# Sample attention's value products moved from ahead of the prompt's attention into two of its steps

## What is computed

```python
logits = jnp.einsum('btngd,btknd->btngk', qg, k_sel) * (HEAD_DIM ** -0.5)
bias = rel_bias[t5_bucket(qpos[None, :, None] - idx)]
logits = jnp.where(valid, logits + bias, -jnp.inf)
p = jax.nn.softmax(logits, axis=-1)
o = jnp.einsum('btngk,btknd->btngd', p, v_sel)
# samples: v_all = concatenate([cache_v[page_table], v]) of 512 + 1 rows, 8 heads, 2 key heads
xs = xs + merge(cy, gc, o, ga, w_out)
```

## Time and profile before

| | us |
|---|---|
| median of 3 runs | 1704.01 |
| lowest, highest | 1702.09, 1707.3 |
| the profiled execution, its own time | 1701.9 |
| span of the profiled execution | 1700.2 |
| PE busy | 1513.3 (89%) |
| DVE, ACT, POOL busy | 1003.3, 697.9, 415.0 |

### The profile page before, as it was taken

One profiled execution on the slowest core, in us unless ns is written; L12 is line 12 of the kernel. 1 busy time (PEld: TensorE's weight loads), 2 busy tenths in 40 slices (PEclk: granted clock), 3 DMA queues, 4 the chain that ended last, 5 costly groups with the idle time before them and its releaser, 6 DMA issues. The chain is left out here.

```text
span 1700.2 us, 28238 instructions
## 1 busy us (share of the span) xinstructions
PE 1513.3 (89%) x10647; PEld 1292.1 (76%) x10647; DVE 1003.3 (59%) x2123; ACT 697.9 (41%) x1238; POOL 415.0 (24%) x270
## 2 busy tenths in 40 slices
PE   5688989989998789999799999999999887569998
PEld 5686979978998769999577777776767665348886
DVE  3342998878988879888443444445455555333222
ACT  4354513253112352232225545556556654344331
POOL 2111224431115803222221001112222233043220
PEclk9999999999999999999879999999999999779999
DMA  7742365221357602224561513511111112295542
GB/s 237 219 107 50 68 92 119 67 75 54 84 161 222 157 22 72 70 75 125 163 156 36 115 37 79 113 35 34 39 45 50 58 61 77 81 231 162 173 149 93
DMA packets 183355, 172.71 MB, mean 102 GB/s; under 512 B 58956, under 2 KB 155348, under 8 KB 182700
## 3 DMA queue, kind: packets, MB, share of 16 engines
q1 hardware_dynamic: 176572, 152.91, 33.7%
q10 hardware_dynamic: 6136, 16.95, 3.4%
q0 software_dynamic: 512, 1.05, 0.2%
HBM read 109.35 MB, written 58.19 MB: 99 GB/s over the span
## 5 line engine op out<-in xcount | busy, mean ns | idle before, releaser
L845 PE MATMUL psum<-xh,wh 128*128 128x384 f32 (+1 forms) x1040 | 345.4, 332 | 23.1 <-ACT hst L782 11.5
L845 PE MATMUL psum<-xl,wh 128*128 128x384 f32 (+1 forms) x1040 | 341.6, 329 | 0.0
L845 PE MATMUL psum<-xh,wl 128*128 128x384 f32 (+1 forms) x1040 | 341.6, 328 | 0.0
L1436 ACT ACTIVATE pts<-psT 128x512 f32<-128x512 f32 (+1 forms) x302 | 167.1, 572 | 255.1 <-PE psT L1717 232.2
L845 PEld LDWEIGHTS psum<-xh,wh 128*128 128x128 f32 x1040 | 197.6, 190 | 26.4 <-ACT hst L782 15.2
L1606 DVE CUSTOM_DVE_ANT_0 L<-psU,mask 128x512 f32<-128x512 f32 (+3 forms) x260 | 143.5, 592 | 114.6 <-PE psU L1711 113.3
L1733 PE MATMUL psO<-pts,vs 128*64 128x128 f32 x2176 | 180.3, 287 | 27.2 <-ACT pts L1436 27.2
L845 PEld LDWEIGHTS psum<-xl,wh 128*128 128x128 f32 x1040 | 197.8, 190 | 0.0
L845 PEld LDWEIGHTS psum<-xh,wl 128*128 128x128 f32 x1040 | 197.5, 190 | 0.0
L995 DVE TENSOR_SCALAR_CACHE_REDUCE hit<-scores,T 128x1792 bf16<-128x1792 f32 (+8 forms) x120 | 184.6, 1538 | 11.7 <-issue 0.9
L693 POOL TENSOR_TENSOR wl<-uw,wh 128x1024 fp32r<-128x1024 f32 x44 | 121.5, 2762 | 276.8 <-ACT wh L730 276.8
(11 more groups left out here) (269 smaller groups left out, 2507.5 us busy)
## 6 DMA issues: line engine op xcount, KB each, us to landing
uw<-in_w_in SPq DMA_DIRECT2D x28, 512.0 KB
uw<-in_w_in SPq DMA_DIRECT2D x32, 256.0 KB
qt<-d_q SPq DMA_DIRECT2D x16, 512.0 KB, 4.0
xst<-in_x_prompt SPq DMA_DIRECT2D x15, 512.0 KB, 4.0
xr<-in_x_prompt SPq DMA_DIRECT2D x15, 512.0 KB, 4.4
out_y_prompt<-fin SPq DMA_DIRECT2D x15, 512.0 KB, 3.0
gate<-d_ga SPq DMA_DIRECT2D x17, 256.0 KB, 4.4
d_mix<-mix SPq DMA_DIRECT2D x17, 256.0 KB, 2.2
```

What stands on the lines that cost most here:

```text
L845: last = nc.tensor.matmul(u[:, 0:k * P], a[:, w % 2, cc, :], x[:, s0:s0 + k, cc, :], start=(cc == 0 and e == 0), stop=(cc == KC - 1 and e ...
L1436: A.activation(out, src, ACT.Copy).then_inc(act_pt, 1)
```

## The change

The 32 products with the cached values leave the prologue. One sequence (four matmuls) is put behind each of the first four groups of keys in step 1, and the other four behind those of step 2. For that:

- the pages of values and the samples' probabilities lie in the convolution's output buffer (`early`, a view of `yc`), which is written by the convolution from DVE's part of step 3 on;
- the samples' results and those of the short tile share bank 0 of `OT`: the own-value product opens it, the short tile's products go to the columns behind with `start=False`;
- the waits `vpad_done`, `som_done` and ACT's for `pe_pv` go; PE's waits for the pages move to the first use in step 1;
- `sample_out` and `finish(0)` go to DVE's part of step 3 (`finish(0)` stood in step 2), behind a new wait for `sample_pv`.

```diff
+SAMPLE_STEPS = (1, 2)
...
-        vpage = L[:, 2:4, :].rearrange("p a b -> p (a b)")[:, 0:NS * NPAGE * 128].rearrange("p (n d) -> p n d", d=128)
+        pages_at = flags_at + LS // 2 + 1
+        vpage = early[:, pages_at:pages_at + NS * NPAGE * 128].rearrange("p (n d) -> p n d", d=128)
+        spts_at = pages_at + NS * NPAGE * 128
+        spts = early[:, spts_at:spts_at + NPAGE * NS * NH].rearrange("p (g x) -> p g x", g=NPAGE)
...
-            act.wait_ge(pe_pv, NS)
-            evac(("sT", 0), pts[:, 0, 0:256], PT[:, pt_no["sT", 0] % 2, 0:256])
+            evac(("sT", 0), spts[:, :, :].rearrange("p g x -> p (g x)"), PT[:, pt_no["sT", 0] % 2, 0:256])
...
-            V.memset(L[:, 0:2, LP:LW], 0.0).then_inc(pad_done, 1)
+            V.memset(L[:, :, LP:LW], 0.0).then_inc(pad_done, 1)
 
             def sample_out():
-                dve.wait_ge(pe_pv, NS + 1)
+                dve.wait_ge(sample_pv, 1)
...
-                V.memset(L[:, 2:4, LP:LW], 0.0).then_inc(vpad_done, 1)
-                dr().then_inc(som_done, 1)
+                dr()
...
-                if p == 0:
+                if p == SAMPLE_STEPS[-1] + 1:
                     sample_out()
+                    finish(0)
...
-                if p >= 2 and pairs[p - 2][1] == GRP - 1:
+                if p > 2 and pairs[p - 2][1] == GRP - 1:
                     finish(tile_no[pairs[p - 2][0]])
...
                         if p == 0:
-                            last = T.matmul(OT[64 * side:64 * side + 64, 0, 0:GRP * LREM], vs[0:rows, b + e, 64 * side:64 * side + 64],
+                            last = T.matmul(OT[64 * side:64 * side + 64, 0, NS * NH:NS * NH + GRP * LREM], vs[0:rows, b + e, 64 * side:64 * side + 64],
...
-                                            start=(b + e == 0), stop=(b + e == nblk(i) - 1))
+                                            start=False, stop=(b + e == nblk(i) - 1), skip_group_check=True)
...
-            pe.wait_ge(vp_in, 16 * hp)
-            pe.wait_ge(vpp_in, 16 * hp)
+
             T.matmul(OT[:, 0, 0:NS * NH], own[:, 128:256], sown[:, :], start=True, stop=False, skip_group_check=True)
-            for b in range(NS):
-                for g in range(NPAGE):
...
+            def sample_products(bs):
+                for b in bs:
+                    for g in range(NPAGE):
+                        last = T.matmul(OT[:, 0, b * NH:(b + 1) * NH], vpage[:, b * NPAGE + g, :],
+                                        spts[:, g, b * NH:(b + 1) * NH], start=False,
+                                        stop=(b == NS - 1 and g == NPAGE - 1), skip_group_check=True)
+                if NS - 1 in bs:
+                    last.then_inc(sample_pv, 1)
...
-            pe.wait_ge(vpad_done, 1)
...
-                    pe.wait_ge(som_done, 1)
...
                     products(p, *g)
+                    if p in SAMPLE_STEPS and e < NS // len(SAMPLE_STEPS):
+                        if (p, e) == (SAMPLE_STEPS[0], 0):
+                            pe.wait_ge(vp_in, 16 * hp)
+                            pe.wait_ge(vpp_in, 16 * hp)
+                        sample_products([SAMPLE_STEPS.index(p) * (NS // len(SAMPLE_STEPS)) + e])
```

More of the change, by code:

```diff
@@ L1159, in attend_and_convolve @@
     t_no = {j: n for n, j in enumerate(tjobs)}
-    pv_after = lambda p: NS + 1 + sum(len(groups(x)) for x in range(p + 1))
+    pv_after = lambda p: NS + sum(len(groups(x)) for x in range(p + 1))
     tile_no = {i: n for n, i in enumerate(TILE_ORDER)}
@@ L1238, in attend_and_convolve @@
         vpp_in = sem("vpp_in")
-        spick_done, som_done, pad_done, vpad_done = sem("spick_done"), sem("som_done"), sem("pad_done"), sem("vpad_done")
+        spick_done, sample_pv, pad_done = sem("spick_done"), sem("sample_pv"), sem("pad_done")
         q16_zero, mix_zero, b16_in = sem("q16_zero"), sem("mix_zero"), sem("b16_in")
@@ L1467, in _ @@
                     n = t_no[job]
-                    act.wait_ge(pe_pv, NS + 1 + max(0, n - 2))
+                    act.wait_ge(pe_pv, NS + max(0, n - 2))
                     m = sides(p) * k * P
@@ L1567, in finish @@
                     dve.wait_ge(pe_pv, pv_after(0))
-                    TT(mix[:, s, :, 0:LREM], OT[:, s, 0:GRP * LREM].rearrange("p (c t) -> p c t", t=LREM), gate[:, s, :, 0:LREM], ALU.mult)
+                    TT(mix[:, s, :, 0:LREM], OT[:, s, NS * NH:NS * NH + GRP * LREM].rearrange("p (c t) -> p c t", t=LREM), gate[:, s, :, 0:LREM], ALU.mult)
                     TT(mix[:, s, :, SROW:SROW + NS], som[:, :, :], gate[:, s, :, SROW:SROW + NS], ALU.mult)
@@ L1773, in _ @@
             pe.wait_ge(act_pt, act_copies(("sP", 0)))
-            pe.wait_ge(vp_in, 16 * hp)
-            pe.wait_ge(vpp_in, 16 * hp)
             T.matmul(OT[:, 0, 0:NS * NH], own[:, 128:256], sown[:, :], start=True, stop=False, skip_group_check=True)
-            for b in range(NS):
-                for g in range(NPAGE):
-                    last = T.matmul(OT[:, 0, b * NH:(b + 1) * NH], vpage[:, b * NPAGE + g, :],
-                                    pts[:, 0, g * 64 + b * NH:g * 64 + (b + 1) * NH], start=False,
-                                    stop=(b == NS - 1 and g == NPAGE - 1), skip_group_check=True)
-            last.then_inc(pe_pv, 1)
+            def sample_products(bs):
[6 more added lines that the diff above has]
+                    last.then_inc(sample_pv, 1)
             pe.wait_ge(v_in, 32)
             pe.wait_ge(pad_done, 1)
-            pe.wait_ge(vpad_done, 1)
             for p, (i, j) in enumerate(pairs):
```

## The result

The changed kernel takes 1711.6 us (median of 8 runs, 1708.64 to 1718.77) against 1703.39 us (8 runs) of the kernel before beside it: 8.2 us more, ratio 1.0047, 95% interval [1.003, 1.0063]. That is slower, by more than the 0.3% that can be told from no change. The forecast was 1705.5 us and the range ended at 1711.0. Two further sets gave 1.0052 [1.0035, 1.0069] and 1.0053 [1.0033, 1.0073].

What follows compares the result with a forecast made beforehand. PE was taken to bound steps 1 and 2. The terms -5.8 (gain) + 0.3 (clock) + 7.0 (steps) gave +1.5 us: 1703.4 against the profiled execution, 1705.5 against the median; range 1701.5 to 1711.0.

Steps and rivals of the forecast that it cites:

- What bounds: Steps 1 and 2: PE is busy 13.33 of 13.80 and 15.33 of 15.80 us, so added records cost full time outside gaps.
- the mask as the next wait: Start of step 1: without the products DVE waits for POOL's mask with bias, until 869.2 instead of 862.7.
- third rival: Start of step 1: mask is not the next wait, PE gains 12.5 us, net -5.6 us, 1698.4; chance 0.05.
- What the steps pay: Steps 1 and 2: each of eight sequences costs 0.88 us at full clock, 7.0 us together.
- second rival: Steps 1 and 2: weight loads slip into PE's gaps, steps pay 4.3 us, net -1.2, 1702.8; chance 0.10.
- The gain of 5.8 us less 0.3: Step 0's transposes on PE start 5.8 us sooner, less 0.3 us lost while the clock is still low.
- What is late next: Prologue's end: POOL's mask holds DVE's first piece of step 1 to 869.2 instead of 875.27, a 6.1 us gain.
- The way from DVE to PE: Step 1: PE waits for DVE's first release near 869.9, then four half-clock pieces take 3.4 us; transposes start about 873.1.
- first rival: Steps 1 and 2: the clock falls, each low stretch loses 1.7 us; 0.38 for some fall, 0.18 for three or more.
- 0.20 for slower: Whole kernel slower beyond 0.3%: 0.18 for three or more low clock stretches plus 0.02 for the late release.
- The small edits: Removed waits, longer clearing of `L`, moved page waits, DVE's copies and `finish(0)`: cost nothing.
- the moved release: `tile_done` of the short tile comes about 20 us later; tile number 2's mask keeps 9 us to spare, costing nothing.

Runs made afterwards that it cites:

- the mask first: Changed kernel with the loads of tile number 1 (queries, gate, mask) issued ahead of SP's page loads: 1704.61 us, ratio 0.9997 to the kernel before.
- look_before_3: One more profiled execution of the kernel before, no edit: third stage 648.6 us, head of step 3 at 81.51 us.
- products_ahead: Changed kernel's layout, but the 32 products back ahead of the first step as in the kernel before: 1706.04 us, ratio 1.0003 to the kernel before.
- every_other: Changed kernel with one sequence behind every second group of keys (0, 2, 4, 6) of steps 1 and 2: 1709.18 us, ratio 1.002 to the kernel before.
- two_per_group: Changed kernel with all eight sequences in step 1, two behind each of its first four groups: 1716.59 us, ratio 1.0062 to the kernel before.
- in_gap: Changed kernel with all 32 products in step 1's logits, between the first and second head's pieces: 1706.16 us, ratio 1.001 to the kernel before.
- look_after_3: One more profiled execution of the changed kernel, no edit: third stage 653.8 us, head of step 3 at 87.65 us.

## Why the prediction was wrong

**What bounds, and the mask as the next wait: right.** DVE started at POOL's end within 0.04 us, PE stood idle 8.7 us (I wrote some 5, as I had not counted that its four pieces ran at full clock, and the mask was later). Putting the mask first brought DVE 6.8 us forward. So the third rival (mask not next) was rightly put aside.

**What the steps pay, 7.0 us: right.** 7.1 us, 0.90 a sequence, and 6.9 us less with 31 products left out. The Trainium skill (TensorE: Matmul & The Clock Gate, Part 2, Step-by-step) says that PE pulls weight loads ahead of matmuls in flight; I had worked out 4.3 us from it, an estimate. Here the gap of 0.17 us ahead of the samples' loads stayed, as between the kinds of matmul in the earlier trace rows, and only the one behind them went. The measured 7.1 us decide against that estimate for this pattern, and the second rival (loads in the gaps) fell.

**The gain of 5.8 us less 0.3: the term that failed.** It failed at its root, in "What is late next": "the removed 13.3 us bring DVE 875.27 - 869.2 = 6.1 us". In the first pair of profiles DVE's first piece came 4.6 us sooner, and over all nine (four of before, five of the change) 3.5: 43.6 us into the stage before, 40.1 with the change. The way from DVE to PE was right: I took 0.6 us off, and step 2's logits begin 50.3 us into the stage against 53.2, a gain of 2.9, where 5.5 had been forecast. (By its own terms PE's start was 869.9 + 3.4 = 873.3 and not 873.1, which is 0.2 us.)

Of the missing 2.6 us, 1.8 are on the side of the change: POOL's mask was ready 40.1 us into the stage and not 38.3. I took one DMA's 5.6 us from issue to POOL as its length ("POOL gets it at 863.08"). In the other eight profiles of the two kernels it was 6.45 to 7.63 us, so that was the shortest, and in the mean of the change it was 1.6 us longer; the rest is its issue. The other 0.8 are on the side of before: its products are not always 13.3 us long. In look_before_3 they took 10.5, since the clock fell only 3.7 us into the block and in the other three profiles within 0.7, and PE reached step 1's logits 39.8 us into the stage instead of 42.9; in products_ahead the block took 10.8 us.

So the mechanism was right and a size was wrong: the sum with the measured terms is -2.9 + 7.1 = +4.2 us, and not +1.5. The 8 us that were measured are more than this too. One fall of the clock in five profiles adds 0.6 in the mean, which makes the 4.9 us of the third stage; what lies beyond is the open part below. And with the products left out altogether the mean span of 24 runs is 1703.9, as before within 0.7 us, so over all runs the prologue gives back from 0 to 3 us for the 7.1 that the steps pay. I had forecast that the two nearly cancel. That the sign of the sum came out right is no merit, for a sum of +1.5 was called no change.

**The clock in steps 1 and 2, the first rival: half right.** The fall exists and follows how dense the small matmuls stand (none in steps 1 and 2 in the one profile of every_other, one of 2.95 us in five profiles of the change, 9.5 us of loss in the one profile of two_per_group). I had it at 0.38 for some fall, and placed one or two falls in "no change" on the strength of the +1.5; with the gain at 2.9 the sum starts from +4.2, and a single fall carries it past 5.1. The fault in the numbers is this link: I priced the rival from a centre that rested on the luckiest of nine DMAs, and its low end left no room for a smaller gain, so the 0.20 for slower was too low. That the throttled state is the default and activity releases it (the Trainium skill, TensorE: Matmul & The Clock Gate, Part 1, What's actually happening) fits the pauses: in the profile of the change PE was idle from 868.4, the clock was at the lower level from 871.4 to 881.7, and PE's matmuls took 0.63 us again from 877.69 on. It does not by itself give the prologue of before, where PE was busy for 13 us at 0.53.

**The small edits and the moved release: right.** Layout 1.0003; the slack was 11 us, where I had worked out 9.

**What stays open.** The third stage accounts for 4.9 us and the profiles' spans for 6.7 (standard error 1.5); all runs give 7.4 (0.7), the medians 8.2 to 8.9. The other two stages, which nobody edited, hold the 1.8 us between the first two of these numbers, and they are within chance. The profiled executions are shorter than the mean of all runs for both kernels, by 3.0 us for the change and 2.2 for before, so the profiles may leave out some of the loss. More falls in the timed runs would fit, and so would a quicker prologue of the kernel before in them; without a trace of these neither is shown. Why the gain of the profiles without the products (2.6 to 3.9 us at the head of step 3) is absent from the means of their runs is the same question.

## What to carry to other kernels

Work that is hidden under a wait is free only as long as the wait is there: taking 13 us of products out of a prologue bought 3 to 4 us at best, since the mask behind them was only 2 to 6 us from being the next wait in the four profiles, while the same products cost their full 7 us where PE was the bound. Ask first what comes next, and repair that first: one line in SP's order was worth 9 us to the changed kernel, and only with it did a new place for the products come out, narrowly, ahead of the old one. And where a gain is the difference of two ends, read both ends from more than one execution: a DMA's landing wandered by 2 us here, and a block of small matmuls by 3.

## What the runs showed of the hardware

- DVE's scaling of 128x2064 f32 took 1.29 to 1.30 us in 15 profiles, and 3.34, 3.86 and 3.81 us in the three in which it began while POOL's addition ran; it ended 1.08 to 1.10 us after POOL's each time, and POOL's kept its length, 4.08 us. That remainder is most of the 1.29 us that the scaling takes alone, so it did not run slowly beside POOL, it stood. The row shows no idle time for this: the instruction itself looks long. The Trainium skill (SBUF — State Buffer, SBUF: two separate sides) says that the port pair shared by the two engines is an exclusive lock, and that the loser waits the whole instruction out. The numbers agree. This wait ate some 2 us of what the mask first brought.
- PE's clock can be at the lower level while PE counts as busy. In the block of 64 records of 8 columns the clock was at 0.53 in the mean in before and at 0.66 in in_gap; with 16 such records at a time in step 1 it was at 0.53 for 22 us, and the same loads went from 1.86 us to 3.49; with 8 at a time it fell in one profile of five. The other work beside them then pays as well: 9.5 us in two_per_group. That the block started the fall in the prologue is not shown: the clock fell 0.65 us into it in before, and in look_after_3, which has no block, it was at 0.50 from 861.2 to 878.1, the same place in the stage.
